# Position bias prepared beside the first projections, and one scores step moved in the choice

## The reference, cut to what matters

```
z = h @ w_in_a ; q, k, v, xr, gr = split(z)
logits = q.k * scale + rel_bias[t5_bucket(dist)][head] ; masked where dist < 0
w = softmax(map 1) - lam * softmax(map 2) ; o = w @ v          # prompt
same with k, v = paged cache + the new token                   # the 8 samples
x = x + concat(norm(o), rglru(conv(xr)) * gelu(gr)) @ w_out_a
x = x + peer(rmsnorm(x)):  q = x @ w_q ; s = q . sub_keys ; top 16 of s1 + s2 per head
        y = sum_k softmax(s)_k * gelu(x . u[e_k]) * v[e_k]
```

## Time and profile before

| | |
|---|---|
| runs, median (lowest to highest) | 3589.25 us (3589.11 to 3593.84) |
| the profiled execution, its own time | 3586.5 us |
| its span in the trace | 3584.7 us |
| granted TensorE clock, mean over the span | 0.936 of 2.4 GHz |
| PE, DVE, ACT, POOL busy | 87%, 74%, 11%, 46% of the span |
| projections up to the last block | 34 to 207 us |
| between projections and attention | 207 to 222 us |
| attention | 222 to 614 us |
| choice, layer 0 | 709 to 1009 us |

### The profile page before, as it was taken

How to read it: one execution, slowest core, us unless ns; L and a number is a source line. 1 busy time by engine, 2 the same in 40 slices (tenths; PEclk the granted TensorE clock), 3 DMA queues, 4 the chain that set the end, 5 groups by cost and what they waited for, 6 DMA issues and landing times.

```text
span 3584.7 us, 58142 instructions
## 1 busy us (share of the span) xinstructions
PE 3131.5 (87%) x17422; PEld 2034.7 (57%) x17422; DVE 2649.7 (74%) x5876; ACT 410.8 (11%) x960; POOL 1658.0 (46%) x1447
## 2 busy tenths in 40 slices
PE   6958888997279999999999899894399999999997
PEld 3542113486256666666665685692266666666654
DVE  5947775267978888888877421389888888988777
ACT  1011112011111100000000100111111100000000
POOL 3726662011037766666666100011066656667664
PEclk9969999998589999999999999996699999999999
DMA  6878885212059999999999516322099999999998
GB/s 215 286 143 307 319 306 184 112 51 91 36 218 410 410 405 410 407 403 410 409 410 410 191 71 48 121 86 83 26 408 410 409 410 410 403 410 410 409 410 331
DMA packets 299952, 1021.21 MB, mean 285 GB/s; under 512 B 57805, under 2 KB 59253, under 8 KB 296638
## 3 DMA queue, kind: packets, MB, share of 16 engines
q0 software_dynamic: 188928, 687.95, 50.1%
q1 hardware_dynamic: 84928, 324.07, 23.1%
q10 hardware_dynamic: 25982, 7.72, 2.4%
HBM read 1013.90 MB, written 5.72 MB: 284 GB/s over the span
## 4 chain that ended last, share of the span: by engine, by line
PE 52%; DMA 17%; DVE 16%; issue 10%; POOL 3%; ACT 1%; DVEq 1%; POOLq 0%; SPq 0%; ACTq 0%; PEldq 0%
PE ps L971 11%; PE ps L962 11%; PE ps L696 7%; DMA hn<-peer_v_in,area 7%; PE ps L708 6%; PE ps L866 5%; PE ps L784 4%; DMA hn<-peer_u_in,area 3%; DMA area<-peer_v_in,area 3%; PE ps L905 2%; DMA area<-peer_u_in,area 2%; PE ps L878 2%; POOL area L612 2%; DVE area L1705 2%; DVE hn L1816 1%
## 5 line engine op out<-in xcount | busy, mean ns | idle before, releaser
L971 PE MATMUL ps<-area 128*128 128x512 f32 x2048 | 945.5, 605 | 37.6 <-DVE area L1799 36.0
L612 POOL DMA_INDIRECT area<-peer_u_in,area x396 | 511.7, 1292 | 898.5 <-DVE area L1811 278.7
L962 PE MATMUL ps<-hT,area 128*128 128x256 f32 x4096 | 925.5, 379 | 0.0
L962 PEld LDWEIGHTS ps<-hT,area 128*128 128x128 f32 x4096 | 778.2, 190 | 214.6 <-issue 121.9
L612 POOL DMA_INDIRECT area<-peer_v_in,area x396 | 453.2, 1144 | 363.3 <-DVE xs L1816 154.7
L971 PEld LDWEIGHTS ps<-area 128*128 128x128 f32 x2048 | 374.7, 191 | 420.5 <-issue 418.2
L1811 DVE CUSTOM_DVE_ANT_0 area<-area,hn 128x1024 f32<-128x1024 f32 x384 | 458.4, 1225 | 41.0 <-DMA area<-peer_u_in,area 34.0
L905 PE MATMUL ps<-area 128*128 128x32 bf16 x6144 | 196.3, 179 | 175.8 <-DVE area L1705 175.6
L905 PEld LDWEIGHTS ps<-area 128*128 128x128 bf16 x6144 | 188.7, 99 | 213.2 <-issue 188.4
L1816 DVE SCALAR_TENSOR_TENSOR hn<-area,hn 128x1024 f32<-128x1024 f32 x192 | 246.1, 1282 | 47.1 <-DMA area<-peer_v_in,area 43.8
L1816 DVE SCALAR_TENSOR_TENSOR xs<-area,xs 128x1024 f32<-128x1024 f32 x192 | 246.4, 1283 | 42.5 <-DMA area<-peer_v_in,area 27.1
(11 more groups left out here) (260 smaller groups left out, 3045.8 us busy)
## 6 DMA issues: line engine op xcount, KB each, us to landing
area<-peer_ut_in SPq DMA_DIRECT2D x256, 512.0 KB, 8.7
area<-peer_v_in SPq DMA_DIRECT2D x256, 512.0 KB, 6.8
area<-wq_in SPq DMA_DIRECT2D x8, 2048.0 KB, 18.7
area<-w_in_c_in SPq DMA_DIRECT2D x6, 2048.0 KB, 7.9
area<-w_in_a_in SPq DMA_DIRECT2D x5, 2048.0 KB, 10.2
area<-peer_u_in,area POOLq DMA_INDIRECT x396, 10.8
area<-peer_v_in,area POOLq DMA_INDIRECT x396, 11.6
area<-w_out_a_in SPq DMA_DIRECT2D x2, 2048.0 KB, 10.7
```

Of the source, the lines that this page charges most:

```text
L612: pool.indirect_dma_start(ring[r], None, ins[what + str(l)], bass.IndirectOffsetOnAxis(ap=idx[:, i:i + 1], axis=0)).then_inc(rows_landed[r ...
L962: m = pe.matmul(ps[c % 2][:, 0:DT * P], us[c][:, k, :], hT[:, k, 0:DT * P], start=(k == 0), stop=(k == KD - 1))
L971: m = pe.matmul(ps[2 + 2 * t + h][:, :], cT[:, c % 2, t * P:(t + 1) * P], vs[c % 2][:, h * 512:(h + 1) * 512], start=False, stop=False, sk ...
```

## The change

It has two parts. In the first, the bias of the four heads is made during the q, k and v projections: TensorE's two products of heads 0 and 2 stand after the first and second block, those of heads 1 and 3 after the second row tile of the next block; ScalarE does its part at the same places. SyncE only stores `wide` there (between the weight loads), and loads all four tables back after block 3 has been used. ScalarE waits for the store before it reuses `wide`. The constants' six loads are issued before the first projection, the six stores of k, v and state after the transposes. Buffers move so that nothing overlaps: `wide`, `ohs`, `rbx` and `rbw` lie in `grT`, which is written only by the fifth block. In the second, TensorE and ScalarE do the second tile's scores before the queries of the third (both layers).

SyncE, where the weights are loaded:

```diff
-        weight(5)
-
-
-        for h in range(HEADS):
+        def store_wide(h):
             sp.wait_ge(wide_ready, h + 1)
             sp.dma_start(ins["skew"][h], wide).then_inc(stored, 16)
             n_stores[0] += 1
-            sp.wait_ge(stored, 16 * n_stores[0])
+
+        weight(3)
+        store_wide(0)
+        store_wide(1)
+        weight(1)
+        store_wide(2)
+        store_wide(3)
+        weight(1)
+
+        sp.wait_ge(weights_used, 4)
+        sp.wait_ge(stored, 16 * HEADS)
+        for h in range(HEADS):
             n = SEQ + P - 1
             src = bass.AP(ins["skew"].tensor, h * P * n + P - 1, [[n - 1, P], [1, SEQ]])
             sp.dma_start(bias[:, h, :], src).then_inc(bias_landed, 16)
-            sp.wait_ge(bias_landed, 16 * (h + 1))
```

TensorE; the loop over the heads behind `bd` goes, and in `peer` the second tile's scores move:

```diff
+        def head_bias(h):
+
+            if h == 0:
+                pe.wait_ge(scalar_dmas, 16 * 6)
+            pe.wait_ge(act_results, h + 1)
+            for c0 in (0, 320):
+                b = abank()
+                pe.matmul(b[:, 0:min(320, SEQ + P - 1 - c0)], rbw, ohs[:, c0:min(c0 + 320, SEQ + P - 1)],
+                          start=True, stop=True).then_inc(act_bank_full, 1)
...
         natural(abank, act_bank_full, hT, FIRST_ORDER, spread_queries)
-        for _ in range(2):
-            natural(abank, act_bank_full, hT)
+        for h in (0, 2):
+            head_bias(h)
+            natural(abank, act_bank_full, hT, after=lambda: head_bias(h + 1))
         for _ in range(2):
             tlayout(abank, act_bank_full, na)
...
-            q1 = queries(1)
             scores(1, q0)
+            q1 = queries(1)
             q2 = queries(2)
```

ScalarE:

```diff
         act.wait_ge(normed, TILES + 1)
         act.wait_ge(act_bank_full, na[0])
+        act.dma_start(ohd, ins["c_ohd"]).then_inc(scalar_dmas, 16)
+        act.dma_start(rbs, ins["rel_bias"]).then_inc(scalar_dmas, 16)
...
+        def head_bias(h):
+            if h == 0:
+                act.wait_ge(scalar_dmas, 16 * 6)
+            act.wait_ge(act_bank_full, na[0])
+            act.copy(rbw, rbx[:, h:h + 1].broadcast_to([BUCKETS + 1, P])).then_inc(act_results, 1)
+            if h:
+                act.wait_ge(stored, 16 * h)
+            b = take()
+            step(act.copy(wide[:, 0:320], b[:, 0:320]))
+            act.sem_inc(act_bank_free, 1)
+            b = take()
+            act.copy(wide[:, 320:SEQ + P - 1], b[:, 0:SEQ + P - 1 - 320]).then_inc(act_bank_free, 1)
+            act.wait_ge(act_bank_free, na[0])
+            act.sem_inc(wide_ready, 1)
...
+                if j and place == 2:
+                    head_bias(2 * j - 1)
                 b = take()
                 act.copy(z[0:rows(t), t, j * AW:(j + 1) * AW], b[0:rows(t), :]).then_inc(act_bank_free, 1)
+            if j < 2:
+                head_bias(2 * j)
 
         for j in range(2):
+            if j == 1:
+                act.wait_ge(stored, 16 * HEADS)
...
             act.sem_inc(dec_rows_spread, 1)
+            scores(1)
             exps(1, P, PH)
             queries(0)
-            scores(1)
```

```diff
+    A_K = 4 * (TILES + 1) + DEC + 4
-    A_QB = 2 * (TILES + 1) + 3 * (TILES + 1) + 2 * 2 * RB + 2 * TILES + DEC + 1
+    A_QB = 2 * (TILES + 1) + 3 * (TILES + 1) + 2 * 2 * RB + 2 * TILES + DEC + 1 + 2 * HEADS
...
-    bias = at(26400, HEADS, SEQ)
+    bias = at(30496, HEADS, SEQ)
...
-    wide = at(33056, SEQ + P - 1)
+    wide = at(13964, SEQ + P - 1)
```

More of the change, by code:

```diff
@@ L289, in program @@
     obs = hn[0:8, 0:TILES, :].rearrange("p t c -> p (t c)").rearrange("p (b c) -> p b c", b=DEC)
-    bias = at(26400, HEADS, SEQ)
+    bias = at(30496, HEADS, SEQ)
     lg = at(28448, 2, 2, SEQ)
-    wt = at(30496, 2, SEQ)
-    pT = at(31520, SEQ)
-    sq = at(32032, SEQ)
+    wt = at(26400, 2, SEQ)
+    pT = at(27424, SEQ)
+    sq = at(27936, SEQ)
     rs = at(32544, SEQ)
-    wide = at(33056, SEQ + P - 1)
-    ohs = area[0:BUCKETS + 1, 33700:33700 + SEQ + P - 1]
-    rbx = area[0:BUCKETS + 1, 34340:34340 + HEADS]
-    rbw = area[0:BUCKETS + 1, 34350:34350 + P]
+    wide = at(13964, SEQ + P - 1)
+    ohs = area[0:BUCKETS + 1, 14604:14604 + SEQ + P - 1]
+    rbx = area[0:BUCKETS + 1, 15244:15244 + HEADS]
+    rbw = area[0:BUCKETS + 1, 15252:15252 + P]
     bd = hn[:, TILES, 0:(SUB + 1) * 8].rearrange("p (a b) -> p a b", a=SUB + 1)
@@ L481, in program @@
     A_Q = 2 * (TILES + 1) + 2 + DEC
-    A_QB = 2 * (TILES + 1) + 3 * (TILES + 1) + 2 * 2 * RB + 2 * TILES + DEC + 1
+    A_K = 4 * (TILES + 1) + DEC + 4
+    A_QB = 2 * (TILES + 1) + 3 * (TILES + 1) + 2 * 2 * RB + 2 * TILES + DEC + 1 + 2 * HEADS
     A_PEER = 2 * (TILES + 1) + PH + 1 + HC // 4 * (2 * TILES - 1) + DT + 2
-    A_CG = A_QB + 2 * HEADS + 2 * HEADS * TILES + 4 * RB + A_PEER + 2 * (TILES + 1) + 2 * KD
+    A_CG = A_QB + 2 * HEADS * TILES + 4 * RB + A_PEER + 2 * (TILES + 1) + 2 * KD
     A_BG = A_CG + 2 * KD
@@ L742, in _ @@
                 m.then_inc(act_bank_full, 1)
-        pe.wait_ge(scalar_dmas, 16 * 6)
         b = abank()
@@ L748, in _ @@
         m.then_inc(act_bank_full, 1)
[L750 to L755, removed]
         take_turns(3)
@@ L931, in peer @@
                     .then_inc(act_bank_full, 1)
+            scores(1, q0)
             q1 = queries(1)
-            scores(1, q0)
             q2 = queries(2)
@@ L1046, in _ @@
         act.wait_ge(act_bank_full, na[0])
+        act.dma_start(ohd, ins["c_ohd"]).then_inc(scalar_dmas, 16)
+        act.dma_start(rbs, ins["rel_bias"]).then_inc(scalar_dmas, 16)
+        act.dma_start(rb0, ins["rel_bias"][0:1, :].broadcast_to([DEC, HEADS])).then_inc(scalar_dmas, 16)
+        act.dma_start(ohs, ins["c_oh"]).then_inc(scalar_dmas, 16)
+        act.dma_start(rbx[0:BUCKETS, :], ins["rel_bias"]).then_inc(scalar_dmas, 16)
+        act.dma_start(rbx[BUCKETS:BUCKETS + 1, :], ins["c_mask"]).then_inc(scalar_dmas, 16)
+        def head_bias(h):
[12 more added lines that the diff above has]
+            act.sem_inc(wide_ready, 1)
         for j in range(3):
@@ L1070, in _ @@
         act.wait_ge(act_bank_free, na[0])
[L1071 to L1085, removed]
         for t in range(TILES):
@@ L1100, in _ @@
         act.wait_ge(act_bank_free, na[0])
[L1102 to L1115, removed]
+        k3 = outs["k_prompt"].rearrange("(t p) d -> p t d", p=P)
+        v3 = outs["v_prompt"].rearrange("(t p) d -> p t d", p=P)
+        act.dma_start(k3, z[:, 0:TILES, AW:2 * AW]).then_inc(outputs_stored, 16)
+        act.dma_start(v3, z[:, 0:TILES, 2 * AW:3 * AW]).then_inc(outputs_stored, 16)
+        act.dma_start(outs["k_sample"], z[0:DEC, TILES, AW:2 * AW]).then_inc(outputs_stored, 16)
+        act.dma_start(outs["v_sample"], z[0:DEC, TILES, 2 * AW:3 * AW]).then_inc(outputs_stored, 16)
+        act.wait_ge(state_landed, 32)
+        act.dma_start(outs["rgp"], xp[:, :, SEQ:SEQ + RGC - 1]).then_inc(outputs_stored, 16)
+        act.dma_start(outs["rgs"], xd[:, :, :, 1:RGC]).then_inc(outputs_stored, 16)
         def subtract(b_):
@@ L1415, in _ @@
         dve.wait_ge(scalar_dmas, 16 * 6)
+        dve.wait_ge(act_bank_free, A_K)
         q_, k_ = z[0:DEC, TILES, 0:AW], z[0:DEC, TILES, AW:2 * AW]
```

## The result

The median of 8 runs is 3577.26 us (3568.70 to 3582.60), against 3589.11 us of 7 runs of the kernel before, taken beside them. The ratio is 0.9965, with a 95% interval of 0.9952 to 0.9979: the change makes the kernel 12.6 us faster by the ratio, between 7.5 and 17.2 us by its interval. The forecast was 17.5 us faster.

A forecast was written before the change was run, and what follows sets the result against it. It took the bias chain in the idle stretch before attention, then a mixture of engines in one written order, to bound the kernel. 29.8 - 1.3 (9.6 - 8.3) - 11 = 17.5 us gained, forecast 3571.8 us, range 3560 to 3583.5.

The forecast's parts named there:

- Removed, 29.8 us: Attention's start: VectorE's waits of 25.72 us for the heads' bias and 4.07 us for the last table would go.
- Added in the projections, 9.6 us: Projection blocks: each of four heads costs TensorE a 1.3 us wait and 1.25 us of products; bounds 8 to 15 us.
- the slower rival: Projections: waits and thin products bring TensorE's clock to 1.2 GHz; decides above about 17 us lost, up to 3607 us; 4%.
- Gained between the stages, 8.3 us: Between projections and attention: without twelve transfer issues the first copy starts 7.8 us earlier, plus 0.5 us of higher clock.
- The late gathers, 11 us between 0 and 18.8: Attention's start: stores moved there make key gathers late; 11 us is the middle of 6.5 and 15.7 for key 69.
- The rule of the Trainium skill on completion order: Attention's start: completion increments land only after earlier writes of that DMA engine; alone, 15.7 us late and a sum of 12.8.
- The choice, nothing: Second part, scores before queries: VectorE waits for the Gelu, so between -0.6 and +0.6 us in each layer.
- Attention bound by DMA: Rival: the moved stores' 16 us of engine time is paid in attention; gain only 6 to 12 us, 3577 to 3583; 16%.

The follow-up runs named there:

- e6: e2 with the four heads' spread bias columns made once ahead of the second block, so TensorE waits for no copy; 3556.32 us, 0.9910 of the kernel before.
- e9: The changed kernel with ScalarE copying the state into one run per partition before its two stores, at the same place; 3562.07 us, 0.9915 of the kernel before.
- e4: The kernel before, with only the two state stores moved to the end of attention; 3573.01 us, 0.9949 of the kernel before.
- e7: The changed kernel with the small pieces of `rgs` stored a second time, into `skew`; 3590.10 us, 0.9999 of the kernel before.
- e1: The changed kernel with only the two state stores moved from attention's start to its end; 3563.26 us, 0.9921 of the kernel before.
- e2: The changed kernel with the two state stores issued early, after the fourth projection block; 3561.74 us, 0.9917 of the kernel before.
- e5: e2 with the stores of k and v early as well, after the third block; 3563.54 us, 0.9927 of the kernel before.
- e8: e5 with e6's edit, so all stores early and bias columns spread ahead; 3554.91 us, 0.9904 of the kernel before.
- e10: e9 with e6's edit, so packed state stores and bias columns spread ahead; 3555.14 us, 0.9890 of the kernel before.
- e3: The changed kernel with its second part undone, scores after the queries again in both layers; 3574.56 us, 0.9948 of the kernel before.

## Why the prediction came out as it did

The time lay inside the range, on the side forecast, and 5.5 us above the forecast. By its own steps:

- *Removed, 29.8 us*: right. Both waits are gone and the tables had landed.
- *Added in the projections, 9.6 us*: 10.3 by the trace (137.4 less 127.1): products 5.5 (e6), waits 3.1 (e9's 135.7, without dips, less e6's 132.6), one dip 1.7. Products and waits together are 8.6, a microsecond under the term; that a dip of the clock would come with them was left to the slower rival. The 2.0 us by which the first block ended later aren't the change's: it ended 1.5 us later in e4, where the bias stands in its old place, 0.7 in e9 and 4.8 in e7, and these go with how long the clock was low from 53 us on and with the start of the block (34.45 us before, 35.18 in e9, 35.85 in e7).
- *The slower rival, the clock*: its mechanism is there, its price isn't. In six traces with four waits of 0.9 us (the change, e1, e2, e5, e7, e9) there are 1, 2, 2, 1, 2 and 0 dips to the lower level, each of some 3.4 us and 1.7 us of cost, not the 17 us it needed. Each begins about 2 us after one of these waits. Without the waits (before, e4, e6, e8, e10) there is none in the blocks from 64 us on, though e6, e8 and e10 have the same thin products. The low clock from 53 us on, in all of them, has no wait ahead of it: TensorE was working there without a gap, from 48.48 us on at thin products (`8*128`, in the kernel before). The Trainium skill (TensorE: Matmul & The Clock Gate, HAM oscillation) says that repeated idle gaps throttle the clock, in a case with longer waits than these. The traces agree in kind: a third of the waits here were followed by a dip.
- *Gained between the stages, 8.3 us*: 9.6 (from the blocks' end to the copy of `bd` at 221.57 before and 224.18 after: 14.7 and 5.1).
- *The late gathers, 11 us between 0 and 18.8*: this is the term that was mis-sized. It is 15.99 us, and it falls on key 68, not on key 69, from which I had worked out both ends of the 11 us. I took the middle of 6.5 us (the 12.8 us of one gather in the trace) and 15.7 us (all lands when the stores are through). The 12.8 us was no latency: that gather had been issued late in the burst. Its neighbour, the `skew` store, had landed within a microsecond of it, and that pair was the better evidence. With 15.99 in the place of 11 the sum is 12.5 us, and measured is 12.6. With all terms as traced it is 29.8 - 10.3 + 9.6 - 16.0 = 13.1, and the prompt logits start 11.3 us earlier in spite of the first block's 2.0. That 12.5 and 12.6 are so close is in part luck: in this pair of traces 7.2 of the 11.3 us are left at the end of attention and 5.1 at the end of the span, and the interval of the measured gain is 10 us wide.
- *The rule of the Trainium skill on completion order* (DMA: Bandwidth & Descriptors, Queues, rings and completion order) gave 15.7 us for the wait and 12.8 for the sum. That the numbers agree is luck: 15.7 was for key 69. For key 68, on which the wait fell, the same reckoning gave the 18.8 of the upper end, and a sum of 9.7. Measured is 15.99, because the gather landed at 253.24 and not at 254.9, and was wanted at 237.36 and not at 236.1. Nor is what the rule names as the cause, increments waiting for earlier writes, shown to be at work here: from 235 to 245 us the bytes themselves hardly move (8 and 36 GB/s), and the gathers still crawl when the small stores are nearly through (67 GB/s from 245 to 250).
- *The choice, nothing*: right by the trace; e3 shows that it gains nothing and can't exclude a cost of some microseconds.
- *Attention bound by DMA*: the total alone can't exclude it, since 3577.26 us lies at the edge of its 3577 to 3583. The trace speaks against it: the loss is one wait at the start, before the dense stretch, and not a longer stretch. From the first logits to its end attention took 351.2 us with the change, 347.1 before and 344.0 in e2; in e9, without a burst, it took 350.3. These lengths differ between runs by as much as the change could have done there, and nothing finer can be said.

## What to carry to other kernels

When a chain of waits is moved off the path, look at what was running beside it for free. Here a burst of 12-byte stores had the idle stretch to itself, made the chain look longer than it was, and went on to hold up the next stage's gathers. Count a store's pieces, not its bytes, and copy scattered values into one run before storing them. Where a transfer is slow in the trace of before, look when it landed beside the burst, and not only how long it took: that says more of a transfer issued at another time. And price the first transfer behind the burst before the later ones.

## What the runs showed of the hardware that I had not expected

48 KB and 6 KB in pieces of 12 bytes, spread over 16 engines, hold up other transfers for some 20 us: a 0.5 MB gather of 5.9 us takes 21.9, and a 320 KB store of 2.4 us takes 15.0. Gathers behind them hardly move (8 GB/s for all engines together), and they stay slow for some 10 us more when the small pieces are nearly gone (67 GB/s, then 185, then 414). And a transfer in small pieces can block the engine that issues it: the issue of the added one took ScalarE 8.23 us, where the one before it took 1.34.

TensorE's clock falls to half for some 3.4 us after some waits as short as 0.9 us in a stretch that is otherwise dense, in 8 of 24 such waits, and goes up by itself under dense work. It also falls for 7 to 14 us in the first block, where TensorE has no gap at all. A dip after a wait costs 1.7 us a time, and where the dips fall differs from one execution to the next; two kernels that differ by a microsecond or two in such a stretch have to be compared by their pieces.
